# Output-gate projection of an mLSTM moved into its recurrence's half steps, and branch C's SiLU moved into the merge

## What is computed

```
y  = conv(a * sigmoid(gate)) + b_dw;  yc = silu(layer_norm(y, g, b))                 # branch C
h  = (hf + rev(hb))                        # mLSTM, forward and backward, 4 heads x 128
yd = sigmoid(o_pre) * h                    # o_pre = hl @ w_in[:, O columns]           # branch D
z  = sum_i sigmoid(h @ w_gate_i + b_gate_i) * (ys[i] @ w_branch[i])                  # merge
out = z @ w_out
```

## Time and profile before

| | |
|---|---|
| median of three runs | 3564.94 us |
| the profiled execution's own time | 3567.71 us |
| its span | 3565.9 us |
| granted clock of TensorE, mean over the span | 0.958 of full speed |
| busy: PE, DVE, ACT, POOL | 91%, 63%, 49%, 20% |
| D projection, layer 0 | from 522.1 us |
| mLSTM and O projection, layer 0 | 648.26 to 749.68 us |
| merge, layer 0 | 749.68 to 1157 us |
| mLSTM and O projection, layer 1 | 2471.23 to 2550.80 us |
| a weight block's high part on ACT (L587), low part on POOL (L590) | 1.91 us, 4.60 us, means |

### The profile page before, as it was taken

How to read it: one execution, slowest core, us unless ns; L and a number is a source line. 1 busy time by engine, 2 the same in 40 slices (tenths; PEclk the granted TensorE clock), 3 DMA queues, 4 the chain that set the end, 5 groups by cost and what they waited for, 6 DMA issues and landing times. The chain is left out here.

```text
span 3565.9 us, 49308 instructions
## 1 busy us (share of the span) xinstructions
PE 3261.8 (91%) x18708; PEld 2750.8 (77%) x18708; DVE 2262.3 (63%) x3362; ACT 1732.9 (49%) x2169; POOL 704.8 (20%) x531
## 2 busy tenths in 40 slices
PE   7999889899999979999999399899899969999996
PEld 4987569799999757777777388578788757777885
DVE  3685871621222539999999584763313448999998
ACT  3112762422122547777776622754222347777775
POOL 3001012323322112222121100013344301111111
PEclk8999999999999979999999699999999979999998
DMA  7265025312221339999999244122233218999996
GB/s 262 79 168 141 5 77 181 93 50 101 84 92 50 137 116 336 334 330 334 337 334 349 76 101 102 33 97 76 86 112 95 96 72 310 350 343 352 362 359 249
DMA packets 445700, 647.09 MB, mean 181 GB/s; under 512 B 131662, under 2 KB 214078, under 8 KB 438622
## 3 DMA queue, kind: packets, MB, share of 16 engines
q1 hardware_dynamic: 304960, 557.88, 45.2%
q0 software_dynamic: 24096, 79.60, 6.8%
q10 hardware_dynamic: 116480, 7.35, 2.2%
HBM read 625.01 MB, written 27.08 MB: 183 GB/s over the span
## 5 line engine op out<-in xcount | busy, mean ns | idle before, releaser
L954 PE MATMUL ps<-hx,part 128*128 128x384 f32 (+2 forms) x5088 | 977.4, 352 | 16.7 <-POOL part L590 5.5
L954 PEld LDWEIGHTS ps<-hx,part 128*128 128x128 f32 x5088 | 883.5, 190 | 104.7 <-issue 16.9
L1416 PE MATMUL ps<-part,hx 128*128 128x512 f32 x3072 | 748.1, 396 | 19.8 <-DVE hx L2487 11.4
L1416 PEld LDWEIGHTS ps<-part,hx 128*128 128x128 f32 x3072 | 573.3, 189 | 152.4 <-issue 12.9
L2470 DVE TENSOR_TENSOR part<-raw,part 128x2048 fp32r<-128x2048 f32 x256 | 600.6, 2347 | 24.1 <-ACT part L1782 23.2
L1782 ACT ACTIVATE part<-raw 128x2048 fp32r<-128x2048 f32 x256 | 490.6, 1917 | 147.1 <-DMA raw<-in_w_exp_up 63.5
L590 POOL TENSOR_TENSOR part<-raw,part 128x2048 fp32r<-128x2048 f32 x66 | 303.8, 4603 | 638.6 <-ACT part L587 638.4
L1416 PE MATMUL ps<-hx 128*128 128x512 f32 x1536 | 379.6, 395 | 3.8 <-DVE hx L2470 1.3
L1416 PEld LDWEIGHTS ps<-hx 128*128 128x128 f32 x1536 | 286.7, 188 | 77.9 <-issue 7.7
L587 ACT ACTIVATE part<-raw 128x2048 fp32r<-128x2048 f32 x100 | 190.6, 1910 | 277.3 <-PE ps L954 159.9
L2470 DVE TENSOR_TENSOR hx<-raw,hx 128x2048 fp32r<-128x2048 f32 x128 | 294.2, 2298 | 31.0 <-ACT hx L1782 29.5
(11 more groups left out here) (314 smaller groups left out, 3679.6 us busy)
## 6 DMA issues: line engine op xcount, KB each, us to landing
raw<-in_w_exp_gate SPq DMA_DIRECT2D x128, 1024.0 KB, 6.0
raw<-in_w_exp_up SPq DMA_DIRECT2D x128, 1024.0 KB, 6.2
raw<-in_w_exp_down SPq DMA_DIRECT2D x128, 1024.0 KB, 6.6
raw<-in_w_mod SPq DMA_DIRECT2D x48, 1024.0 KB, 5.8
raw<-in_w_in SPq DMA_DIRECT2D x44, 1024.0 KB, 5.8
raw<-in_w_gate SPq DMA_DIRECT2D x32, 1024.0 KB, 5.3
raw<-in_w_branch SPq DMA_DIRECT2D x16, 1024.0 KB, 5.1
area<-rows_d POOLq DMA_DIRECT2D x40, 256.0 KB, 4.5
```

Of the source, the lines that this page charges most:

```text
L954: last = mm(dst, a, b, start=i == 0, stop=i == len(pairs) - 1)
L1416: last = mm(ps[:, bank, :], x, y, start=kh == 0 and a == 0, stop=kh == 1 and a == len(pairs) - 1)
```

## The change

- The groups of the O projection (`o_piece`) go into the half steps 2 to 11, one in each, between `front(i + 1)` and the numerators; in layer 0 two are left for after the loop. All use PSUM bank 0, so each waits for the sigmoid of the one before. The stage of its own and its barrier are gone.
- ACT takes the sigmoid of group i - 2 (`sig_piece`) at the end of half step i, into a `sig_o` that now holds all tiles and lies in branch C's place. Branch C's result goes to DRAM at the stage's start and comes back in the merge; ACT waits for the store in half step 1.
- After the half steps DVE gates each tile in whole (order 2, 1, 3, 0, 4, 5), PE transposes it in four, and ACT, not DVE, copies it out.
- The SiLU of branch C runs in merge iteration 1, one of its four instructions behind each gate's sigmoid. Branch B's result is loaded back in the merge as well.
- In the D projection `turn_rows` and `conv_sum` change places, `copy_rows` comes one group later and the root one earlier.
- The low part of the second O block and of the first merge block are made by DVE instead of POOL. In the last merge iteration DVE makes the low parts of z of k = 4 to 6 between the sums, not behind them. The transposes of the last modulation rows (layer 0) move into the merge.

The diff, cut to its core, without common indentation:

```diff
@@ -49,6 +49,7 @@
 NROW = 3
+O_FROM, O_STEPS = 2, 10
 WB = 2048
@@ -182,6 +183,11 @@
+def o_order(l):
+    return [2, 1, 3, 0, 4, 5][:tiles_out(l)]
@@ -440,7 +446,8 @@
 q_c = lt_c
-sig_o, _ = cut(work, oG, 2, QC)
+sig_o, _ = cut(ys, 2 * FB * TOK, NT, BW)
+modt_m, _ = cut(work, 5 * TOK + 2 * P, P)
@@ -801,6 +808,7 @@
+load(yc_d[:, :, 0:full * P], y_v[2][:, :, 0:full * P]).then_inc(*S("yc_moved", l).by(16))
 for i, (j, d, ch, outs) in enumerate(half_steps(l)):
@@ -815,15 +823,14 @@
             load_rows(io + NROW)
-split.mixers_to(l, S_O + 2)
-st.leave()
+pool.wait_ge(*S("yc_moved", l).at(48))
+st.leave()
+split.mixers_from(l, S_MERGE + 1)
 load(ys[:, FB * TOK:2 * FB * TOK], yb_d).then_inc(*S("parked", l).by(16))
+load(y_v[2][:, :, 0:full * P], yc_d[:, :, 0:full * P]).then_inc(*S("yc_moved", l).by(16))
 if l == 0:
     load_modt(0, 2, 4)
-split.mixers_to(l, S_MERGE + 1)
-pool.wait_ge(*S("parked", l).at(64))
-st.leave()
@@ -1182,7 +1189,7 @@
 project("d_part", D_GROUPS, S("d_out", l), 2,
-        {1: gate_sums, 2: turn_inputs, 3: turn_maxima, 5: turn_rows, 6: conv_sum, 12: conv_squares},
+        {1: gate_sums, 2: turn_inputs, 3: turn_maxima, 5: conv_sum, 6: turn_rows, 12: conv_squares},
         {} if l else {b: lambda at=at: mod_pair(*at) for b, at in MOD_D.items()})
@@ -1206,10 +1213,24 @@
+wo = {}
+def o_piece(g):
+    half, t = g // full, g % full
+    if t == 0:
+        wo[half] = take_split()
+    if g:
+        pe.wait_ge(*S("o_sig", l).at(g))
+    last = token_major(ps[:, 0, 0:QC], wo[half], 0, QC, t)
+    last.then_inc(*(S("o_mm", l).by(1) if t < full - 1 else (ring_used, 1)))
 front(0)
         front(i + 1)
+    if O_FROM <= i < min(O_FROM + 2 * full, len(hs)):
+        o_piece(i - O_FROM)
     if outs:
@@ -1232,32 +1253,15 @@
         last.then_inc(*S("m_outer", l).by(1))
-st.leave()
-def turn_o(g):
-    half, t = g // full, g % full
-    pe.wait_ge(*S("o_gated", l).at(g + 1))
-    if g >= 2:
-        pe.wait_ge(*S("o_out", l).at(g - 1))
-    for b in range(2):
-        last = nc.tensor.transpose(ps[:, 2 + g % 2, b * P:(b + 1) * P],
-                                   hD[:, t, half * QC + b * P:half * QC + (b + 1) * P], ident)
+for g in range(O_STEPS, 2 * full):
+    o_piece(g)
+for k, t in enumerate(o_order(l)):
+    pe.wait_ge(*S("o_gated", l).at(k + 1))
+    if k >= 2:
+        pe.wait_ge(*S("o_out", l).at(k - 1))
+    for b in range(FB):
+        last = nc.tensor.transpose(ps[:, 2 + k % 2, b * P:(b + 1) * P], hD[:, t, b * P:(b + 1) * P], ident)
     last.then_inc(*S("o_turned", l).by(1))
-for half in range(2):
-    w = take_split()
-    for t in range(full):
-        g = half * full + t
-        if g >= 2:
-            pe.wait_ge(*S("o_gated", l).at(g - 1))
-        last = token_major(ps[:, g % 2, 0:QC], w, 0, QC, t)
-        last.then_inc(*(S("o_mm", l).by(1) if t < full - 1 else (ring_used, 1)))
-        if g:
-            turn_o(g - 1)
-turn_o(2 * full - 1)
-if l == 0:
-    turn_modt(4 * KD)
 st.leave()
@@ -1272,6 +1276,8 @@
     pe.wait_ge(*S("ym_lo", l).at(it // 2 + 1))
+    if l == 0 and it == 1:
+        pe.wait_ge(*S("modc_done", l).at(2))
     if l == 0 and it - 1 in MOD_MERGE:
@@ -1284,6 +1290,9 @@
         g += 1
+    if l == 0 and it == 0:
+        pe.wait_ge(*S("z_part", l).at(g - 1))
+        turn_modt(4 * KD)
     if l == 0 and it in MOD_MERGE:
@@ -1626,7 +1635,6 @@
 def conv_silu(j):
-    act.wait_ge(*S("conv_normed", l).at(j + 1))
     fn(y_v[2][:, j, 0:nt], y_v[2][:, j, 0:nt], ACT.Silu, bias=conv_c[:, j, KS + 2:KS + 3],
@@ -1642,11 +1650,18 @@
 copies("d_part", D_GROUPS, S("d_out", l), 2,
-       {4: gate_exps, 6: copy_rows, 7: lambda: (conv_square(0), conv_square(1)), 8: lambda: conv_square(2), 9: lambda: conv_square(3),
-        14: conv_root})
-for j in range(FB):
-    conv_silu(j)
-st.leave()
+       {4: gate_exps, 7: lambda: (copy_rows(), conv_square(0), conv_square(1)), 8: lambda: conv_square(2),
+        9: lambda: conv_square(3), 13: conv_root})
+st.leave()
+def sig_piece(g):
+    half, t = g // full, g % full
+    if t < full - 1:
+        act.wait_ge(*S("o_mm", l).at(half * (full - 1) + t + 1))
+    else:
+        act.wait_ge(ring_used, ORD[l]["in", S_O + half] + 1)
+    fn(sig_o[:, t, half * QC:(half + 1) * QC], ps[:, 0, 0:QC], ACT.Sigmoid).then_inc(*S("o_sig", l).by(1))
@@ -1656,8 +1671,6 @@
         last.then_inc(*S("m_gate", l).by(1))
-    if i == 5:
-        split.mixers_to(l, S_O + 2)
     if i < 2 * NT - 2:
@@ -1666,19 +1679,19 @@
         last.then_inc(*S("m_kw", l).by(1))
-st.leave()
-for g in range(2 * full):
-    half, t = g // full, g % full
-    if t < full - 1:
-        act.wait_ge(*S("o_mm", l).at(half * (full - 1) + t + 1))
-    else:
-        act.wait_ge(ring_used, ORD[l]["in", S_O + half] + 1)
-    if g >= 2:
-        act.wait_ge(*S("o_gated", l).at(g - 1))
-    fn(sig_o[:, g % 2, :], ps[:, g % 2, 0:QC], ACT.Sigmoid).then_inc(*S("o_sig", l).by(1))
-    if t == full - 1 and not half:
-        split.mixers_to(l, S_O + 3)
+    if i == 1:
+        split.mixers_to(l, S_O + 2)
+        act.wait_ge(*S("yc_moved", l).at(48))
+    if O_FROM <= i < min(O_FROM + 2 * full, 2 * NT):
+        sig_piece(i - O_FROM)
+for g in range(O_STEPS, 2 * full):
+    sig_piece(g)
+split.mixers_to(l, S_O + 3)
+for k, t in enumerate(o_order(l)):
+    act.wait_ge(*S("o_turned", l).at(k + 1))
+    last = fn(y_v[3][:, :, t * P:(t + 1) * P], ps[:, 2 + k % 2, :].rearrange("p (b n) -> p b n", b=FB), ACT.Copy)
+    last.then_inc(*S("o_out", l).by(1))
 st.leave()
@@ -1704,9 +1717,15 @@
         last.then_inc(*S("z_gate", l).by(1))
+        if it == 1:
+            if j == 0:
+                act.wait_ge(*S("yc_moved", l).at(64))
+            conv_silu(j)
         if j == 0 and it % 2 == 0:
                 act.wait_ge(ring_used, ORD[l]["branch", it - 1] + 1)
+            else:
+                act.wait_ge(*S("parked", l).at(64))
             if it == 2 * NBR - 2:
@@ -2190,8 +2209,7 @@
 for j in range(FB):
-    V.tensor_tensor(y_v[2][:, j, 0:nt], y_v[2][:, j, 0:nt], cstd[:, 0:nt], ALU.mult
-                    ).then_inc(*S("conv_normed", l).by(1))
+    V.tensor_tensor(y_v[2][:, j, 0:nt], y_v[2][:, j, 0:nt], cstd[:, 0:nt], ALU.mult)
 st.leave()
@@ -2279,18 +2297,15 @@
     divide(i)
-st.leave()
-for g in range(2 * full):
-    half, t = g // full, g % full
-    dve.wait_ge(*S("o_sig", l).at(g + 1))
-    c = hD[:, t, half * QC:(half + 1) * QC]
-    V.tensor_tensor(c, c, sig_o[:, g % 2, :], ALU.mult).then_inc(*S("o_gated", l).by(1))
-    dve.wait_ge(*S("o_turned", l).at(g + 1))
-    V.tensor_copy(y_v[3][:, 2 * half:2 * half + 2, t * P:(t + 1) * P],
-                  ps[:, 2 + g % 2, 0:QC].rearrange("p (b n) -> p b n", b=2)).then_inc(*S("o_out", l).by(1))
-if l == 0:
-    take_modt(2, 4)
+    if i == 2:
+        split.mixers_from(l, S_O + 1)
+        split.mixers_to(l, S_O + 2)
+for k, t in enumerate(o_order(l)):
+    dve.wait_ge(*S("o_sig", l).at(full + t + 1))
+    dve.wait_ge(*S("m_num", l).at(2 * full))
+    V.tensor_tensor(hD[:, t, :], hD[:, t, :], sig_o[:, t, :], ALU.mult).then_inc(*S("o_gated", l).by(1))
+split.mixers_to(l, S_MERGE + 1)
 st.leave()
@@ -2323,11 +2338,13 @@
                 z_low(j)
+                if j:
+                    z_low(FB + j - 1)
         g += 1
+    if l == 0 and it == 0:
+        take_modt(2, 4).then_inc(*S("modc_done", l).by(1))
     if l == 0 and it in MOD_MERGE:
         move_mod(MOD_MERGE[it])
-for k in range(FB, KD - 1):
-    z_low(k)
 st.leave()
```

More of the change, by code:

```diff
@@ L154 @@
 o_turned z_part z_sum z_hi z_lo ym_hi ym_lo p_y xn xn_hi h2_tmp xn_T left_in aff_out picked r_logits r_aff r_affT r_slotT g_out g_mm e_acc e_hid e_turned e_hH e_hL
-e_yH e_yL e_comb var std conv_sig conv_cent conv_var conv_std conv_normed m_abs m_log m_exps m_gate
+e_yH e_yL e_comb var std conv_sig conv_cent conv_var conv_std m_abs m_log m_exps m_gate
 p_var p_std z_gate r_cent r_exp e_sil q_mu q_std v_std v_nb xhat_n conv_part ab_part d_part ab_out d_out
@@ L712, in load_modt @@
                             at = (2 * (v - v0) + s) * KD
-                            load(modt[at:at + KD, :], mod_d[layer, s, row * D:(row + 1) * D].rearrange("(k n) -> k n", n=P)
+                            load((modt if l else modt_m)[at:at + KD, :], mod_d[layer, s, row * D:(row + 1) * D].rearrange("(k n) -> k n", n=P)
                                  ).then_inc(*S("modt_in", l).by(16))
@@ L990, in turn_modt @@
                     pe.wait_ge(*S("modt_in", l).at(2 * rows))
-                    nc.tensor.transpose(ps[:, 4, 0:rows], modt[0:rows, :], ident[0:rows, 0:rows]
+                    nc.tensor.transpose(ps[:, 4 if l else 3, 0:rows], (modt if l else modt_m)[0:rows, :], ident[0:rows, 0:rows]
                                         ).then_inc(*S("mod_turned", l).by(1))
@@ L1887, in take_modt @@
                         last = V.tensor_scalar(modc[:, v, :, :].rearrange("p k s -> p s k"),
-                                        ps[:, 4, (v - v0) * 2 * KD:(v - v0 + 1) * 2 * KD].rearrange("p (s k) -> p s k", s=2),
```

(1 more changed line is left out.)

## The result

The changed kernel takes **3548.5 us** (median of six runs, 3543.0 to 3552.7) beside 3565.3 us of the kernel before on the same chip (3562.6 to 3574.8): a ratio of 0.9948, with a 95% interval of 0.9934 to 0.9962. It is faster by 0.5%. It is where rival 2 was priced (3550 us), to which I had given a chance of 0.07. The profiled run took 3548.55 us, its span 3546.7 us, 19.2 us less than before.

A forecast was written before the change was run, and what follows sets the result against it. The prediction took most of the program as bound by PE, busy for 91% of the span. Its terms, -4.5 - 9.3 - 1.3 + 2.0 + 12.0 + 4.3 = +3.2, gave 3567.7 + 3.2 - 2.8 = 3568 us, range 3553 to 3586.

The forecast's parts named there:

- rival 2: Half steps: sigmoid's table loads while ACT still waits for the group; ring 7.6 us, 14 us less, 3550 us; chance 0.07.
- the term of the half steps: mLSTM with O groups in its half steps: longer than the two stages before, by 2.0 us in layer 0, 12 in layer 1.
- the ring: Half steps: waits from O group through sigmoid, exponentials, key copies and key transposes to the next group; 8.9 us, two table loads included.
- the store of branch C in layer 1: Second half step of layer 1: ACT waits for branch C's result to reach DRAM, taken as 8.1 us.
- D projection, doors, end of the merge: PE waits removed: layer 0's D projection, 4.5 us; the mLSTM's start in both layers, 9.3 us; layer 0's merge end, 1.3 us.
- Layer 0, 103.4 us: Layer 0 from the mLSTM's start to the merge's: 103.4 us against 101.4 before, a loss of 2.0 us.
- Layer 1, 91.4 us: Layer 1 from the mLSTM's start to the merge's: 91.4 us against 79.6 before, a loss of 12 us.
- The clock, +4.3 us: Half steps: PE's clock falls behind three of about 11 gaps of 1.9 us, 1.44 us each; loss 4.3 us, bounds 0 and 16.
- SiLU in the merge, 0: Merge: SiLU and two table loads, 3.3 us, fit into 3.5 us spare in layer 1; cost 0, up to 3.
- Rival 1: Half steps: the clock falls at most of the 11 gaps; with all 11, 3580 us; chance 0.25.
- Rival 3: Half steps: rings bound by PE, or a shorter tail; 3560 us and below, down to 3555; chance 0.12.
- rivals 4 and 5: Late weights in layer 1 or the slow store, 3575 us, chance 0.05; a drain at each table switch, 3598 us, chance 0.03.

The follow-up runs named there:

- e1: The changed kernel with a second, needless wait ahead of every O-group sigmoid, so its table load comes behind the wait for the group; 3573.6 us, 1.0016 of the kernel before.
- e5: The kernel before with only the D projection's reordering (turn_rows and conv_sum swapped, row copy and root moved along); 0.9986 of the kernel before.
- e7: The kernel before with e5's table, e6's SiLU and the low parts of z between the sums, without O groups in the half steps; ratio 0.9956.
- e6: The kernel before with only branch C's SiLU moved into the merge's second iteration; 0.9971 of the kernel before.
- e4: The changed kernel with every O-group sigmoid one half step later and, in layer 0, the merge's first weight split earlier; 3531.6 us, 0.9899 of the kernel before.
- e2: The changed kernel with Copy in place of the O groups' sigmoids, so 31 table loads fall away and the output is wrong; 0.9920 of the kernel before.
- e9: e4 with e1's second wait added, so each sigmoid's table load carries the wait for its group; 0.9889 of the kernel before.
- e10: e4 with three of layer 1's four tiles gated by DVE ahead of the last division instead of behind it; 0.9895 of the kernel before.
- e3: The changed kernel with branch C's SiLU back at the end of the D projection, ahead of the barrier; 0.9971 of the kernel before.
- e8: The kernel before with a one-column Copy on ACT at the O projection's start, taking the barrier's wait from the first sigmoid; one run, 3578.8 us.

## Why the prediction was wrong

**The step that failed** is in the term of the half steps: the first 1.29 in the ring's sum, sigmoid's table load behind the wait for the group, and with it the reason given against rival 2, "ahead of L1679 ACT waited 12.58 us for PE and only then loaded". The row is right. But I took it for what a load does, and it is what happens to a load whose activation has a second wait, here the barrier's. The rings' sigmoids are inside a stage and have one wait: their load runs ahead of it, and the distance was 7.61 us instead of 8.9. A second term of the sum failed beside it, the store of branch C in layer 1, which took 4.6 us and not 8.1 (below). Both cases stood in the trace of the kernel before. In its timeline of ACT two of the first loads run at once, and their activations then wait, one of them for PE:

```profile
8.64 1.28 ACT L1459 ACT_TABLE_LOAD   x1
20.48 0.20 ACT L1459 ACTIVATE stat<-stat 128x1 f32<-128x1 f32 x1 [10.56 <-DVE stat L1859]
...
75.36 1.28 ACT L1522 ACT_TABLE_LOAD   x1
97.52 0.60 ACT L1522 ACTIVATE area<-ps 128x512 f32<-128x512 f32 x1 [20.88 <-PE ps L954]
```

The groups of lines would have shown it too: how long ACT idles ahead of all loads of a line. This row is the changed kernel's, 17 loads and 0.3 us:

```profile
L1664 ACT ACT_TABLE_LOAD x17 | 21.8, 1283 | 0.3
```

and this one e1's:

```profile
L1665 ACT ACT_TABLE_LOAD x17 | 21.8, 1283 | 63.8 <-PE ps L961 63.8
```

Point by point:

- *D projection, doors, end of the merge*: right, each within 0.3 us, in the traces and in e5 to e7. The value weights did move along. (The exponentials end at 572.55 us, not 572.8, which changes nothing.)
- *The ring*: its form (through ACT's order, released by the key copies) and all its other terms were right; 7.57 us without the one load stands beside 7.61 measured, and 8.86 with it beside 8.95 in e1. The "11" gaps and rings of the clock and of rival 2 are ten in the sum's own working, six in layer 0 and four in layer 1, and ten in the traces.
- *Layer 0, 103.4 us*: 94.1. With the load where I had put it, e1 has 109.9; without its three slow groups (1.5 each) that is 105.4. Of the last 2 us one is at the end, where I had no more loads between the last sigmoids, which e1's order has. The other is ahead of group 0, which ends 15.6 us after the stage's start and not 14.6, because the clock fell in the third half step (last section).
- *Layer 1, 91.4 us*: 81.35, and 91.43 in e1. That agreement is luck. The store of branch C took 4.6 us, not 8.1 (below, its row among the DMA issues), so that the third key copies came 5.4 us after the stage's start instead of 8.9, and the cold clock that I had put behind that gap didn't come: group 0 ends at 10.0 us, not 15.0. In e1 three later slow groups make up for these 5 us. In the changed kernel they are half of the 10 us by which this stage was missed; the other half is the loads.

```profile
yc_d<-area POOLq DMA_DIRECT2D x1, 1024.0 KB, 4.6
```

- *The clock, +4.3 us*: mis-sized, since the gaps it was counted for didn't come. Where they did come, in e1, six groups were slow, not three. The price was right (4.61 - 3.12 = 1.49 for 1.44). The changed kernel has one slow group, behind a gap of 2.29 us in layer 1, and low clocks at the end of each stage and into the merge, which the sum had no term for.
- *SiLU in the merge, 0*: right. PE has no idle time between the merge's blocks, and e6 keeps all of the doors' gain.
- *Rival 2* is what happened, with its mechanism: 14 us less than the sum, and the clock's 4.3 with it, is -15; measured -19. That its price came so near is in part luck: it was short of the store's 5 us. *Rival 1* is what e1 shows in part. *Rival 3* had the time (3555 to 3560) nearer than the forecast, but not the cause: the changed kernel's rings are not PE-bound, e4's are. Of *rivals 4 and 5* nothing is seen.

The Trainium skill (ScalarE: Activation LUTs, "What ACT_TABLE_LOAD costs") has 1283 ns for the load, as all 17 of L1664 and all of e1's show, and a drain of 1380 ns beside it. No row here has room for the drain: from load to sigmoid it is 1.29 us in e1. Its advice to batch by set ("Table sets: the hidden batching unit"), which I took as speaking against this change, would have been worth at most the 10 us of e2, which leaves the sigmoids out altogether; with all loads kept, the later sigmoids and the early split were worth 17 (e4).

e1, the kernel that the sum described, lands at +0.16%, beside the forecast of +0.09%. That bears out the rings and their loads, but not every term: the 5 us too many ahead of layer 1's first group stand against slow groups that cost 9 us instead of 4.3. Of the 22 us between forecast and result 19.5 are in the two stages and 2.4 in the clock.

## What to carry to other kernels

Before a table load goes into a sum, look whether ACT idles ahead of it or behind it, over all loads of the program, and how many waits its activation has: with one, the load hides in the wait; with two, it can come behind one of them. And when an engine alternates between a chain that others wait for and a piece that itself waits, put that piece behind the next link of the chain: here this was worth as much as taking the table loads away in layer 0, and 4.6 us more in layer 1.

## What was not expected of the hardware

In e1 the same gap of 1.85 us on PE, in rings with the same instructions, was followed by a slow group three times and by a fast one three times. The stretches of three of layer 0's rings (the clock is the third number from the end):

```profile
670.20:680.70 10.50, 8.63 (x61) 8.45 (x61) 3.92 (x14) 5.25 (x11) 2.37 (x3) 0.84 0.21 52
680.70:691.10 10.40, 8.55 (x60) 8.36 (x60) 3.38 (x11) 5.25 (x11) 2.38 (x3) 0.84 0.22 50
691.10:700.10 9.00, 7.14 (x61) 6.96 (x61) 3.47 (x11) 5.25 (x11) 2.38 (x3) 1.00 0.27 61
```

Between the second row and the third nothing in PE's work differs. The second key transposes of layer 0 show the same across kernels whose instructions are the same up to there. PE idles 1.90 us ahead of them in the changed kernel and 1.91 in e1, and these are the stretches behind:

```profile
642.70:645.40 2.70, 2.70 (x26) 2.70 (x25) 1.40 (x5) 2.70 (x9) 2.33 (x3) 1.00 0.85 211
643.40:647.70 4.30, 4.30 (x26) 4.30 (x25) 2.99 (x7) 4.30 (x11) 2.41 (x4) 0.60 0.85 237
```

The same 26 matmuls take 2.7 us there and 4.3 here. In e2, e4, e9 and e10 the clock falls at this place as in e1, in e6 and e7 it doesn't. So layer 0's stages of e1, e2, e4 and e10 hold some 1.2 us that the changed kernel's 94.1 us lack, and the gains of e2, e4 and e10 over it are that much understated. The length of a gap alone does not tell whether the clock falls behind it; behind 0.51 us no ring's group was slow, behind 1.85 half of them (over both layers), and a sum should keep both ends there. The first groups of layer 1's merge are the other case: 24 us in the changed kernel, e4 and e9, 24.9 in e10, 22 in e1, e2, e3, e5 to e8 and before. No run here tells what decides it.
